# A decoder step with 32 experts: rows of the expert matrices dealt to the partitions in blocks of eight

## The chip, the cores and the metric

The kernel runs on one core of one Trainium2 chip. The metric is the device time of one execution in microseconds (us), taken as the median of several runs. TensorE is written PE, its weight load PEld, VectorE DVE, ScalarE ACT, GpSimd POOL and the engine that issues most DMAs SP.

## The reference, cut to what matters

One step of a decoder trunk: 256 prompt tokens and 8 sample tokens, 264 in all, of width 1024. Attention and a gated linear attention come first, then a mixture of experts with 32 experts, of which each token uses 4. All numbers are float32. What bears on the change is the expert part:

```python
def expert_ffn(xb, w_gu, b_gu, w_d, b_d):
    gu = xb @ w_gu + b_gu                 # xb (rows, 1024), w_gu (1024, 2048)
    gate, up = jnp.split(gu, 2, axis=-1)
    gate = jnp.minimum(gate, SWIGLU_LIMIT)
    up = jnp.clip(up, -SWIGLU_LIMIT, SWIGLU_LIMIT)
    glu = gate * jax.nn.sigmoid(SWIGLU_ALPHA * gate)
    return ((up + 1) * glu) @ w_d + b_d   # w_d (1024, 1024)
```

Both products sum over 1024 rows of a weight matrix. The order in which these rows are taken does not matter, as long as the other operand is taken in the same order.

## The kernel before, in words

The program is written engine by engine, with semaphores. A first phase (to about 424 us of the trace) computes attention and the projections, with the layer's other weights. The second phase is the expert part, and all of its weights, 32 x 12 MB, pass once through `ring`, six slots of 2 MB in SBUF.

**Loads.** SP issues them (`load_expert`, L1719 to L1732): for each expert four loads of `w_gu` and two of `w_d`, 2 MB each, in the order in which PE uses them. Each waits at `slots_used` until PE has finished with the slot. The 1024 rows of a matrix are cut as "(k p)": block k holds 128 consecutive rows, one to a partition. A `w_gu` load takes two blocks, so a partition gets two separate rows of 8 KB; a `w_d` load takes four blocks, so a partition gets four separate rows of 4 KB.

**Routing.** After the second norm (`normed`, L1192 to L1206) the activations stand in `hT` with the 1024 features on the partitions. PE turns them into token rows (L737 to L742, the helper `transpose` at L337), in six banks of PSUM, two of which are in use in turn, and ACT copies each bank to `tok` (`copy_out`, L1061 to L1063 and L953). In PE's order behind these turns come the small matmuls that count the tokens of each expert (L744 to L755), which DVE waits for to make `pick` (`set_pick`, L1535 to L1543), the 0/1 matrix that says which token stands in which of an expert's 64 places.

**Experts, in pairs.** `gather` (L771 to L779) multiplies `tok`, 128 features at a time, with `pick` and so gives `xg`, the tokens of two experts with the features on the partitions. `gate_up` (L786 to L813) multiplies `xg` with the `w_gu` slots: two column halves of the array work at once, one for gate and one for up. DVE and ACT make the SwiGLU (`swiglu`, L1554 to L1566) and leave it in `hid`, 64 rows of 1024 features. `turn_hidden` (L815 to L823) turns it: eight matmuls, each with 128 columns of `hid` as weights and the 64 x 64 identity as moving operand. ACT copies the result to `hidT` (L1080). `down` (L833 to L847) multiplies `hidT` with the `w_d` slots; `combine` (L849 to L857) puts the rows back to their tokens and DVE adds them to `acc` (L1572). PE's order is written out by hand in `pair` (L859 to L888), so that the steps of one expert stand between the matmuls of another.

**The end.** A last norm (L1638 to L1646), turns, and the stores of y.

A float32 matmul shows in the trace as two instructions of weight load and two of matmul; a `transpose` shows as one of each.

Of the kernel before, what the change touches and what calls it, by code (L numbers as in the profile page):

```python
# [29 lines left out]
ACT = mybir.ActivationFunctionType  # L30
AX_X = mybir.AxisListType.X

P = 128
D = 1024
KT = D // P
# [9 lines left out]
NE, TOPK, FF = 32, 4, 1024  # L45
CAP = 64
# [34 lines left out]
def decoder_step(nc, x_prompt, x_sample, c_prompt, c_sample, cache_k, cache_v, cache_logf, state_gla,  # L81
# [4 lines left out]
    with ExitStack() as ctx:  # L86
# [7 lines left out]
        ps = ctx.enter_context(nc.psum_tensor("ps", [P, 8, 512], F32))  # L94
# [19 lines left out]
        tok = sb("tok", [P, 3, D])  # L114
# [67 lines left out]
        hid = part(zone, slice(0, CAP), 4160, FF)  # L182
# [60 lines left out]
        scalar_full, scalar_free = sem("scalar_full"), sem("scalar_free")  # L243
# [9 lines left out]
        v_index, a_index, q_index = {}, {}, {}  # L253
# [47 lines left out]
        def _(pe):  # L301
# [41 lines left out]
            bank = vector_bank()  # L343
# [3 lines left out]
            bank = vector_bank()  # L347
            for k in range(KT):
                ins = transpose(bank[:, 9 * k:9 * k + 9], c_rows[:, k * P:(k + 1) * P])
# [3 lines left out]
            for k in range(KT):  # L353
                bank = vector_bank()
                for t, (t0, tn) in enumerate(TOK_TILES):
                    ins = transpose(bank[:, t0:t0 + tn], tok[0:tn, t, k * P:(k + 1) * P])
# [36 lines left out]
            bank = vector_bank()  # L393
            for t, (t0, tn) in enumerate(TOK_TILES):
                ins = pe.matmul(bank[:, t0:t0 + tn], ones[0:tn, :], rstd_diag[0:tn, t, 0:tn],
                                start=True, stop=True)
# [35 lines left out]
            bank = vector_bank()  # L432
            from_scalar("q3")
            for i in range(4):
                ins = transpose(bank[0:NS, i * P:(i + 1) * P], qT[:, i, TP:T])
# [12 lines left out]
            for name, src in (("k", kT), ("v", vT)):  # L448
                from_scalar(f"{name}3")
                for t, (t0, tn) in enumerate(TOK_TILES):  # L450
                    bank = vector_bank()
                    for i in range(4):
                        ins = transpose(bank[0:tn, i * P:(i + 1) * P], src[:, i, t0:t0 + tn])
# [4 lines left out]
            bank = vector_bank()  # L458
            for t, (t0, tn) in enumerate(TOK_TILES):
                transpose(bank[0:tn, t * HA:(t + 1) * HA], fT[:, t0:t0 + tn])  # L460
            for t in range(2):
                ins = transpose(bank[:, (3 + t) * HA:(4 + t) * HA], neg_cum[0:HA, t * P:(t + 1) * P])
# [3 lines left out]
            bank = vector_bank()  # L466
            pe.matmul(bank[:, 0:HA * NS], ones[:, :], qk_new.rearrange("p a b -> p (a b)"), start=True, stop=True)
            ins = pe.matmul(bank[:, HA * NS:2 * HA * NS], ones[0:NS, :], f_diag.rearrange("p a b -> p (a b)"),
                            start=True, stop=True)
# [62 lines left out]
            for i in range(2):  # L532
                bank = vector_bank()
                vector_filled(pe.matmul(bank[:, 0:T], w_alpha_sb[:, i * P:(i + 1) * P], alrT[:, :],
                                        start=True, stop=True), f"alpha{i}")
            for c in range(NCH):
                bank = scalar_bank()
                for h in range(HB):
                    ins = transpose(bank[0:CH, h * DV:(h + 1) * DV], vbT[:, h, c * CH:(c + 1) * CH])
                scalar_filled(ins, f"vb_tok{c}")  # L540
            bank = vector_bank()
            for h in range(HB):
                ins = transpose(bank[0:NS, h * DV:(h + 1) * DV], vbT[:, h, TP:T])
# [6 lines left out]
            for i in range(2):  # L550
                for f in range(2):
                    half = slice(64 * f, 64 * f + 64)
                    bank = vector_bank()
                    for c in range(NCH):
                        ins = pe.matmul(bank[0:CH, c * CH:(c + 1) * CH], e_k[half, i * NCH + c, :],
                                        e_q[half, i * NCH + c, :], start=True, stop=True)
# [3 lines left out]
            bank = vector_bank()  # L560
            for h in range(HA):
                ins = transpose(bank[:, h * 64:(h + 1) * 64], lf_rows[:, h:h + HA * (PAGE - 1) + 1:HA])
# [4 lines left out]
            for i in range(2):  # L567
                bank = scalar_bank()
                for c in range(NCH):
                    ins = transpose(bank[0:CH, c * P:(c + 1) * P], al_d[:, i * NCH + c, :])  # L570
                scalar_filled(ins, f"kd_tok{i}")
            from_scalar("kd_tok1")
            for i in range(2):
                for c2 in range(2):
                    bank = vector_bank()
                    for c in (2 * c2, 2 * c2 + 1):
                        ins = pe.matmul(bank[:, (c % 2) * 256:(c % 2) * 256 + 256], kd_tok[:, i, c, :],
                                        vb_tok[:, c, i * 256:(i + 1) * 256], start=True, stop=True)
# [5 lines left out]
            for h in range(HB):  # L584
                i, f = h // 2, h % 2
                bank = vector_bank()
                for c in range(NCH):
                    ins = pe.matmul(bank[:, c * CH:(c + 1) * CH], vb_tok[:, c, h * DV:(h + 1) * DV],
                                    A_T[:, i, f, c * CH:(c + 1) * CH], start=True, stop=(c == 0))
                    if c:  # L590
                        ins = pe.matmul(bank[:, c * CH:(c + 1) * CH], gla_S[:, c - 1, i, :],
                                        qe[:, f, i * NCH + c, :], start=False, stop=True)
# [4 lines left out]
            bank = vector_bank()  # L597
            vector_filled(pe.matmul(bank[:, :], ones[:, :], past_lf.rearrange("p a b -> p (a b)"),
                                    start=True, stop=True), "page_sums")
            bank = vector_bank()  # L600
# [16 lines left out]
            for b in range(NS):  # L617
                if b in (3, 6):
                    gate_tile()
                bank = vector_bank()  # L620
# [5 lines left out]
            bank = vector_bank()  # L626
            out = bank[:, 0:64].rearrange("p (i f b) -> p i f b", i=2, f=2, b=16)[:, :, :, 0:NS]
            for b in range(NS):
                for i in range(2):
                    ins = pe.matmul(out[:, i, :, b], state[:, b, i, :], qb_new[:, i, b, :],  # L630
                                    start=True, stop=True)
# [5 lines left out]
            for h in range(HB):  # L637
                bank = vector_bank()
# [5 lines left out]
            bank = vector_bank()  # L644
# [3 lines left out]
            bank = vector_bank()  # L648
# [3 lines left out]
            bank = vector_bank()  # L652
# [33 lines left out]
            bank = vector_bank()  # L686
            for i in range(4):
                ins = transpose(bank[:, i * NS:(i + 1) * NS], o_rows[:, i * P:(i + 1) * P])
# [6 lines left out]
            for m in range(KT):  # L695
                for n, src in enumerate((oT[:, :, :], obT)):
                    bank = vector_bank()
                    for k in range(4):
                        ins = pe.matmul(bank[:, 0:T], wb[n][:, k, m * P:(m + 1) * P], src[:, k, :],  # L699
                                        start=(k == 0), stop=(k == 3))  # L700
# [8 lines left out]
            for m in range(KT):  # L709
                bank = vector_bank()  # L710
                for k in range(KT):
                    ins = pe.matmul(bank[:, 0:T], wo[k // 4][:, k % 4, m * P:(m + 1) * P], hT[:, k, :],  # L712
                                    start=(k == 0), stop=(k == KT - 1))
# [12 lines left out]
            bank = vector_bank()  # L726
            for k in range(KT):
                pe.wait_ge(sig("h2T"), k + 1)
                ins = pe.matmul(bank[0:NE, 0:T], w_r[:, k, :], hT[:, k, :], start=(k == 0), stop=(k == KT - 1))
            vector_filled(ins, "logitsT")  # L730
            from_vector("logitsT")
            bank = vector_bank()
            for t, (t0, tn) in enumerate(TOK_TILES):
                ins = transpose(bank[0:tn, t * NE:(t + 1) * NE], logitsT[:, t0:t0 + tn])
            vector_filled(ins, "logits")

            for t, (t0, tn) in enumerate(TOK_TILES):  # L737
                for g in range(2):
                    bank = scalar_bank()
                    for k in range(4):  # L740
                        ins = transpose(bank[0:tn, k * P:(k + 1) * P], hT[:, 4 * g + k, t0:t0 + tn])
# [3 lines left out]
            bank = vector_bank()  # L745
# [69 lines left out]
            def turn_hidden(n, j, first):  # L815

                pe.wait_ge(sig("hid_ready"), 2 * n + j + 1)
                if not first:
                    pe.wait_ge(sig("turn_read"), 3 * n + j)
                for k in range(KT):  # L820
                    ins = pe.matmul(ps[:, 4, k * CAP:(k + 1) * CAP], hid[:, k * P:(k + 1) * P],  # L821
                                    ident[0:CAP, 0:CAP], start=True, stop=True)
                ins.then_inc(sig("turned"), 1)  # L823

# [101 lines left out]
        def _(act):  # L926
# [21 lines left out]
            def copy_out(dst, name, rows=P, cols=T, func=ACT.Copy, scale=1.0):  # L948
                bank = take(name)
                src = bank[0:rows, 0:cols]  # L950
                if len(dst.shape) == 3:
                    src = src.rearrange("p (a b) -> p a b", b=dst.shape[2])
                nc.scalar.activation(dst, src, func, scale=scale).then_inc(scalar_free, 1)  # L953
# [106 lines left out]
            squares_and_root("x1", "x1_sq", "x1_ss", "x1_rms")  # L1060
            for t, (t0, tn) in enumerate(TOK_TILES):  # L1061
                for g in range(2):
                    copy_out(tok[0:tn, t, g * 512:(g + 1) * 512], f"h2_tok{t}{g}", rows=tn, cols=512)  # L1063
            act.wait_ge(sig("top_shift"), 1)
            nc.scalar.activation(logits, logits, ACT.Exp).then_inc(sig("top_exp"), 1)

# [583 lines left out]
        def _(sp):  # L1650
# [62 lines left out]
                    store(logf_prompt[0, 0].rearrange("(t p) h -> p t h", p=P), f_tok[:, 0:2, :])  # L1713
                    store(logf_sample[0].rearrange("b s h -> (b s) h"), f_tok[0:NS, 2, :])

            gu = w_gu[0].rearrange("e (k p) c -> e p k c", p=P)
            dn = w_d[0].rearrange("e (k p) c -> e p k c", p=P)

            def load_expert(kind, e, number, edge, phase_one=False):  # L1719

# [119 lines left out]
```

## Time and profile before

| what | value |
|---|---|
| median of 3 runs | 1529.31 us (1526.75 to 1529.6) |
| span of the profiled execution | 1524.6 us |
| own time of the profiled execution | not given apart from its span |
| PE busy | 1426.3 us, 94% |
| PE weight load busy | 714.7 us, 47% |
| DVE, ACT, POOL busy | 472.4, 197.6 and 25.3 us |
| mean granted clock of PE | 0.961 of 2.4 GHz |
| DMA | 497.75 MB, mean 326 GB/s |

The span runs from the first to the last instruction of the profiled execution; the runs' times also hold what lies around it, 4.7 us if the profiled execution is like the median run. "Busy" for PE counts pipelined matmuls, which overlap, so 94% says that PE hardly stands still, and not that it works at its peak. The time lies in two phases: about 424 us of the first, and from there to 1524.6 us the routing, the experts and the end.

### The profile page before, as it was taken

The page shows a single profiled execution, that of the slowest core. Times are in us where ns is not written, and L with a number is a line of the kernel's source. Part 1 is how long each engine was busy: PE and PEld are TensorE (multiplying, and loading weights), DVE is VectorE, ACT ScalarE, POOL GpSimd, SP SyncE. Part 2 cuts the span into 40 slices and gives each one's busy share as a digit, 9 for nine tenths or more (in the row PEclk, how much of TensorE's full clock was granted, in tenths as well). Part 3 has the DMA queues.
Part 4 walks back from the last instruction along what each step waited for, and adds up shares of the span by engine and source line. Part 5 has one row for each costly group of instructions (what it writes and reads, how often), then busy time and mean ns, then how long its engine had stood idle before and what let it go on. Part 6 is the DMA issues. An engine that isn't in the chain of part 4 may idle for free.

```text
span 1524.6 us, 17634 instructions
## 1 busy us (share of the span) xinstructions
PE 1426.3 (94%) x6765; PEld 714.7 (47%) x6765; DVE 472.4 (31%) x919; ACT 197.6 (13%) x334; POOL 25.3 (2%) x53
## 2 busy tenths in 40 slices
PE   5999789997979999999999999999999999999996
PEld 2876457645853443434344343443434344343433
DVE  3278764412232141221223122141221322222133
ACT  1022400200120111011011111111101011111112
POOL 0000010210000000000000000000000000000000
PEclk9999967998978999999999999999999999999998
DMA  9935754788426898999999999899998989989980
GB/s 355 332 119 197 284 177 155 275 326 336 133 103 268 366 418 366 364 416 364 420 365 397 382 365 418 365 419 364 364 417 363 418 366 380 400 363 418 367 324 30
DMA packets 103927, 497.75 MB, mean 326 GB/s; under 512 B 6257, under 2 KB 6367, under 8 KB 68016
## 3 DMA queue, kind: packets, MB, share of 16 engines
q1 hardware_dynamic: 100464, 486.77, 80.0%
q0 software_dynamic: 3152, 10.37, 1.9%
q8 instruction: 24, 0.39, 0.1%
q10 hardware_dynamic: 272, 0.09, 0.0%
q14 instruction: 15, 0.12, 0.0%
HBM read 493.86 MB, written 3.35 MB: 326 GB/s over the span
## 4 chain that ended last, share of the span: by engine, by line
PE 85%; DVE 7%; DMA 4%; issue 2%; ACT 2%; DVEq 0%; ACTq 0%; SPq 0%
PE ps L805 29%; PE ps L844 15%; PE ps L776 9%; PE ps L410 9%; PE ps L856 5%; PE ps L821 4%; PE ps L794 4%; PE ps L699 2%; PE ps L712 2%; DMA ring<-in_w_in 2%; DMA ring<-in_w_branch 2%; PE ps L337 1%; PE ps L667 1%; DVE ring L1221 1%; DVE zone L1549 1%
## 5 line engine op out<-in xcount | busy, mean ns | idle before, releaser
L805 PE MATMUL ps<-ring,zone 128*64 128x512 f32 x2048 | 471.0, 603 | 0.0
L805 PEld LDWEIGHTS ps<-ring,zone 128*64 128x64 f32 x2048 | 136.8, 137 | 270.3 <-issue 267.9
L844 PE MATMUL ps<-ring,oT 128*64 128x512 f32 x1024 | 226.0, 594 | 0.0
L1557 DVE TENSOR_SCALAR zone<-ps 64x1024 f32<-64x1024 f32 x32 | 38.9, 1217 | 499.7 <-PE ps L805 499.7
L410 PE MATMUL ps<-hT,ring 128*128 128x264 f32 (+2 forms) x672 | 166.6, 407 | 2.8 <-DMA ring<-in_w_in 2.8
L410 PEld LDWEIGHTS ps<-hT,ring 128*128 128x128 f32 (+2 forms) x672 | 129.7, 196 | 41.8 <-issue 9.7
L776 PE MATMUL ps<-zone,tok 128*128 128x128 f32 (+1 forms) x768 | 142.7, 318 | 2.5 <-DVE zone L1541 2.5
L844 PEld LDWEIGHTS ps<-ring,oT 128*64 128x64 f32 x1024 | 72.1, 137 | 138.9 <-issue 137.0
L776 PEld LDWEIGHTS ps<-zone,tok 128*128 128x128 f32 (+1 forms) x768 | 109.0, 195 | 45.3 <-issue 18.2
L1572 DVE TENSOR_TENSOR zone<-zone,ps 128x264 f32<-128x264 f32 x128 | 53.6, 428 | 174.6 <-PE ps L856 173.3
L856 PE MATMUL ps<-zone,v_tok 128*128 128x264 f32 x256 | 74.1, 412 | 24.1 <-DVE zone L1572 22.6
L856 PEld LDWEIGHTS ps<-zone,v_tok 128*128 128x128 f32 x256 | 43.0, 188 | 80.4 <-issue 37.3
L1080 ACT ACTIVATE oT<-ps 128x512 f32<-128x512 f32 x32 | 19.1, 597 | 385.9 <-PE ps L821 385.9
L821 PEld LDWEIGHTS ps<-ident,zone 64*128 64x128 f32 x512 | 59.4, 188 | 19.0 <-issue 19.0
L821 PE MATMUL ps<-ident,zone 64*128 64x64 f32 x512 | 63.9, 275 | 0.0
L794 PE MATMUL ps<-zone 32*64 32x512 f32 x256 | 63.6, 614 | 0.0
L1090 ACT ACTIVATE v_tok<-ps 64x512 f32<-64x512 f32 x64 | 37.8, 591 | 176.5 <-PE ps L844 176.1
L1076 ACT ACTIVATE k_tok<-zone 64x1024 f32<-64x1024 f32 x32 | 33.8, 1057 | 174.1 <-DVE zone L1557 174.1
L1538 DVE COPY zone<-ident 32x64 f32 (+1 forms) x32 | 5.7, 179 | 125.1 <-PE ps L805 125.1
L953 ACT ACTIVATE zone<-ps 128x264 f32<-128x264 f32 (+1 forms) x41 | 15.9, 387 | 186.5 <-PE ps L410 186.5
L1559 DVE TENSOR_SCALAR zone<-ps 64x1024 f32<-64x1024 f32 x32 | 39.2, 1226 | 1.0
L1562 DVE SCALAR_TENSOR_TENSOR zone<-zone 64x1024 f32<-64x1024 f32 x32 | 38.9, 1217 | 1.1
(281 smaller groups left out, 864.4 us busy)
## 6 DMA issues: line engine op xcount, KB each, us to landing
ring<-in_w_gu SPq DMA_DIRECT2D x128, 2048.0 KB, 10.4
ring<-in_w_d SPq DMA_DIRECT2D x64, 2048.0 KB, 12.4
ring<-in_w_ada SPq DMA_DIRECT2D x12, 2048.0 KB, 13.2
ring<-in_w_in SPq DMA_DIRECT2D x8, 2048.0 KB, 16.1
ring<-in_cache_k SPq DMA_DIRECT2D x64, 256.0 KB, 3.6
ring<-in_cache_v POOLq DMA_DIRECT2D x32, 256.0 KB, 6.1
ring<-in_cache_v SPq DMA_DIRECT2D x32, 256.0 KB, 6.2
ring<-in_w_branch SPq DMA_DIRECT2D x2, 2048.0 KB, 22.2
```

Source lines behind the costliest of these rows:

```text
L410: ins = pe.matmul(bank[0:width, 0:T], w[:, k, c0:c0 + width], hT[:, k, :], start=(k == 0), stop=(k == KT - 1))
L776: ins = pe.matmul(out, tok[0:tn, t, k * P:(k + 1) * P], pick[0:tn, t, :], start=(t == 0), stop=(t == 2))
L794: pe.matmul(banks[64 * half:64 * half + CAP, c, :], expert_row[:, j, :], b_gu_rows[:, half * FF + c * 512:half * FF + (c + 1) * 512], star ...
L805: ins = pe.matmul(banks[64 * half:64 * half + CAP, c, :], xg[:, k, j * CAP:(j + 1) * CAP], w[:, kk, half * FF + c * 512:half * FF + (c + 1 ...
L821: ins = pe.matmul(ps[:, 4, k * CAP:(k + 1) * CAP], hid[:, k * P:(k + 1) * P], ident[0:CAP, 0:CAP], start=True, stop=True)
L844: ins = pe.matmul(ps[64 * half:64 * half + CAP, 5, :], hidT[:, k, :], w[:, kk, half * 512:(half + 1) * 512], start=(k == 0), stop=(k == KT ...
L856: pe.matmul(ps[:, 6 + m % 2, 0:T], ye_tok[:, m * P:(m + 1) * P], putT, start=True, stop=True).then_inc(sig("combined"), 1)
L1090: ins = nc.scalar.activation(ye_tok[64 * j:64 * j + CAP, half * 512:(half + 1) * 512], ps[64 * half:64 * half + CAP, 5, :], ACT.Copy)
L1557: V.tensor_scalar(gate_v, ps[0:CAP, 2 * j:2 * j + 2, :].rearrange("p a b -> p (a b)"), LIMIT, None, ALU.min).then_inc(sig("gate_ready"), 1)
L1559: V.tensor_scalar(hid, ps[64:64 + CAP, 2 * j:2 * j + 2, :].rearrange("p a b -> p (a b)"), LIMIT, -LIMIT, ALU.min, ALU.max).then_inc(sig("u ...
L1562: V.scalar_tensor_tensor(out=hid, in0=hid, scalar=1.0, in1=gate_v, op0=ALU.add, op1=ALU.mult)\
L1572: V.tensor_tensor(acc[:, m, :], acc[:, m, :], ps[:, 6 + m % 2, 0:T], ALU.add)\
```

## The change

It has three parts that belong together.

1. **The loads.** The rows of an expert's matrices are cut as "(p k)" in place of "(k p)": partition p holds the eight consecutive rows 8p to 8p + 7. A `w_gu` load of two k then takes two consecutive rows of 8 KB for a partition, 16 KB in a row, and a `w_d` load of four k takes four consecutive rows of 4 KB, also 16 KB in a row. In the compiled program the load of either kind becomes 128 partitions x 4096 elements, in place of 128 x 2 x 2048 and 128 x 4 x 1024. From one partition to the next the address steps by 64 KB in `w_gu` and 32 KB in `w_d`. The number, size and order of the loads and their waits stay.
2. **`tok`.** Block k of `xg` must now hold the features 8p + k. ACT's copies of the turned activations write the features in that order: `by_row` sends feature 128k + 8b + r to place 128r + 16k + b. An instruction reads its 512 numbers from PSUM in a row and writes them to SBUF in steps of 512 B, eight at a time. The slices of `tok` that `gather` reads stay contiguous.
3. **`hid`.** `turn_hidden` takes for block k every eighth column, from k on, as weights: 128 numbers of a partition with a step of 32 B, in place of 128 in a row.

The output of the experts keeps its order, since only rows that are summed over move. PE's, DVE's and POOL's instructions keep their order and shapes.

```diff
@@ turn_hidden
                 for k in range(KT):
-                    ins = pe.matmul(ps[:, 4, k * CAP:(k + 1) * CAP], hid[:, k * P:(k + 1) * P],
+                    ins = pe.matmul(ps[:, 4, k * CAP:(k + 1) * CAP], hid[:, k:FF - KT + k + 1:KT],
                                     ident[0:CAP, 0:CAP], start=True, stop=True)
@@ ACT, after squares_and_root("x1", ...)
                 for g in range(2):
-                    copy_out(tok[0:tn, t, g * 512:(g + 1) * 512], f"h2_tok{t}{g}", rows=tn, cols=512)
+                    by_row = tok[0:tn, t, :].rearrange("p (r k b) -> p k b r", r=KT, k=KT)
+                    act.wait_ge(scalar_full, a_index[f"h2_tok{t}{g}"])
+                    bank = ps[0:tn, (a_index[f"h2_tok{t}{g}"] - 1) % 2, :]
+                    nc.scalar.activation(by_row[:, 4 * g:4 * g + 4, :, :],
+                                         bank.rearrange("p (k b r) -> p k b r", k=4, r=KT), ACT.Copy)\
+                        .then_inc(scalar_free, 1)
@@ SP
-            gu = w_gu[0].rearrange("e (k p) c -> e p k c", p=P)
-            dn = w_d[0].rearrange("e (k p) c -> e p k c", p=P)
+            gu = w_gu[0].rearrange("e (p k) c -> e p k c", p=P)
+            dn = w_d[0].rearrange("e (p k) c -> e p k c", p=P)
```

## Rows read from the trace of the kernel before

**Rows 1.** The page, part 1: busy time, share and instructions of each engine.

```profile
span 1524.6 us, 17634 instructions
PE 1426.3 (94%) x6765; PEld 714.7 (47%) x6765; DVE 472.4 (31%) x919; ACT 197.6 (13%) x334; POOL 25.3 (2%) x53
```

**Rows 2.** Waits in 475:1480, PE alone: engine line <- releaser: us, times, longest.

```profile
PE ps L856 <- DVE zone L1572: 22.6, 14, 1.6
PE ps L767 <- DVE zone L1624: 1.5, 1, 1.5
```

**Rows 3.** Waits of SP's own queue in 500:1480, same columns.

```profile
SPq L1731 <- PE ps L805: 555.1, 119, 6.0
SPq L1731 <- PE ps L844: 298.4, 60, 11.4
```

**Rows 4.** Windows: stretch, us, busy PE PEld DVE ACT POOL, PEclk, DMA share, GB/s.

```profile
500.00:1480.00 980.00, 957.40 (x4631) 409.40 (x4629) 237.57 (x445) 109.88 (x166) 0.00 (x0) 1.00 0.95 386
920.00:950.00 30.00, 28.39 (x130) 10.13 (x126) 10.00 (x24) 2.63 (x4) 0.00 (x0) 1.00 1.02 417
20.00:25.00 5.00, 3.93 (x18) 2.02 (x22) 1.36 (x6) 0.00 (x0) 0.00 (x0) 1.00 1.01 419
```

**Rows 5.** The page, parts 3 and 6: two DMA queues, and the expert loads' issues.

```profile
q1 hardware_dynamic: 100464, 486.77, 80.0%
q8 instruction: 24, 0.39, 0.1%
...
ring<-in_w_gu SPq DMA_DIRECT2D x128, 2048.0 KB, 10.4
ring<-in_w_d SPq DMA_DIRECT2D x64, 2048.0 KB, 12.4
```

**Rows 6.** Line L821, the turn of `hid`: count, ns min/median/max, first and last start.

```profile
L821 PEld LDWEIGHTS ps<-ident,zone x512: 182/188/188, 494.6 to 1485.6; 64*128 64x128 f32 x171
L821 PE MATMUL ps<-ident,zone x512: 272/272/320, 494.6 to 1485.6; 64*128 64x64 f32 x171
```

**Rows 7.** Timeline, 32 gate/up matmuls and one turn of `hid`: start, us, what.

```profile
917.12 7.09 PE L805 MATMUL ps<-ring,zone 128*64 128x512 f32 x32
...
949.24 1.86 PEld L821 LDWEIGHTS ps<-ident,zone 64*128 64x128 f32 x16 [0.34 <-issue]
```

**Rows 8.** Tile gla_S at L337, weights with a step of 8 floats; its timeline; its window.

```profile
L337 PEld LDWEIGHTS ps<-ident,gla_S x8: 182/203/204, 195.0 to 195.8; 64*128 64x128 f32 x8
...
195.05 0.96 PEld L337 LDWEIGHTS ps<-ident,gla_S 64*128 64x128 f32 x8
...
195.00:196.00 1.00, 1.00 (x10) 0.95 (x8) 0.84 (x2) 0.00 (x0) 0.00 (x0) 0.50 0.00 0
```

**Rows 9.** Lines L667 (weights with a step) and L674 (in a row), and their timeline.

```profile
L667 PEld LDWEIGHTS ps<-ring,dec_scores x128: 91/99/138, 282.8 to 331.3; 128*8 128x8 f32 x128
L674 PEld LDWEIGHTS ps<-tok,small x16: 86/90/90, 290.7 to 333.1; 128*8 128x8 f32 x16
...
325.28 0.14 PEld L667 LDWEIGHTS ps<-ring,dec_scores 128*8 128x8 f32 x7 [0.34 <-issue]
...
326.13 0.09 PEld L667 LDWEIGHTS ps<-ring,dec_scores 128*8 128x8 f32 x1 [0.34 <-issue]
```

**Rows 10.** The chain of waits from 431.98 to 439.46: start, us, what.

```profile
431.98 0.61 ACT tok L953
...
433.32 0.61 ACT tok L953
...
433.97 1.09 PE ps L337 x8
435.06 0.14 PE ps L750 x2
...
439.46 15.03 PE ps L776 x48
```

**Rows 11.** Timeline of ACT, the third pair of copies; a later gather on PE.

```profile
434.61 1.08 ACT L953 ACTIVATE tok<-ps 8x512 f32<-8x512 f32 x2 [0.20 <-PE ps L337]
...
957.71 8.51 PE L776 MATMUL ps<-zone,tok 128*128 128x128 f32 x48
```

**Rows 12.** Windows, columns as in rows 4: the first gather and what follows it.

```profile
440.00:450.00 10.00, 10.00 (x35) 7.53 (x33) 0.78 (x4) 0.60 (x1) 0.00 (x0) 0.50 0.00 0
450.00:460.00 10.00, 10.00 (x29) 4.79 (x30) 0.00 (x0) 1.88 (x2) 0.00 (x0) 0.50 0.01 2
```

## The prediction

> **What bounds the kernel now.** I read the engine shares first, then the waits of the expert phase, then its windows. PE is busy for 94% of the span and no other engine for more than 31% [rows 1]. That alone would allow for a phase in which the DMAs are the bound, so the waits of the experts' stretch come next. From 475 to 1480 us PE's matmuls wait for another unit 15 times, 24.1 us in all, each time for DVE; no DMA stands in that list [rows 2]. The opposite holds: SP, which issues the loads, waits 555.1 + 298.4 = 853.5 of 980 us for PE to give slots back [rows 3]. The loads follow PE, not PE the loads.
>
> How near the loads are to being the bound is in the windows [rows 4]. Over 980 us the experts take 386 GB/s with the DMA engines busy at a share of 0.95; where the engines are full (share 1.02) they move 417 GB/s, and 419 GB/s near the start, with rows of 8 KB that lie 24 KB apart. So PE asks for 386 / 417 = 93% of what the DMAs give. The stretch is PE's, with some 7% in hand for the DMAs: a faster load buys nothing, a load slower by more than 7% costs.
>
> **The change part by part.** The sum is made against the profiled execution, whose span is 1524.6 us; the median of the runs is 1529.31 us. I put the difference of 4.7 us down to what lies around the span and add every term to the median. About 3 us, 0.2%, is what a measurement of this kernel can tell from no change; the three runs lie 2.85 us apart.
>
> *Loads: 192 instructions, neither more nor fewer, same order, same waits.* There are 128 + 64 of 2 MB each [rows 5], 402.7 MB. Their pieces grow from 8 KB and 4 KB to 16 KB. If the longer pieces are moved faster, the gain lies beside PE's work: each load lands earlier in a slot that PE comes to later, and SP's 853.5 us of waiting grow. Worth 0 us, and the cover is PE itself; nothing in this change shortens PE's work, so the cover stays. If they are moved slower, up to 7% is hidden too. The trace holds 24 packets of 16 KB, code loads on queue 8: 0.39 MB in 0.1% of 16 engines' span, which by the rounding is anything between 0.5 and 1.5 us for one [rows 5]. At 417 GB/s over 16 engines, 16 KB take 0.63 us. That row is too coarse and lies on another queue, so the near rows are the two at 417 and 419 GB/s, which agree although in one the rows stand 24 KB apart and in the other they follow each other. I take 0, with +28 us as the far end (a rate 10% lower, worked out under the rivals). Below nothing the reason above excludes a gain.
>
> *The turn of `hid`: 512 weight loads and 512 matmuls [rows 6], all on PE, all on the path.* This is the term to look at hardest, because PE has no slack. One turn is 16 weight loads in 1.86 us [rows 7]: less the last one's own 0.188 us, (1.86 - 0.188) / 15 = 0.111 us from one to the next, or 0.87 ns for each of 128 columns. The weight load sets this pace and not the matmul: 32 matmuls of 512 columns, two at a time, take 7.09 us [rows 7], which is 0.44 us for 512 columns and 0.055 us for the 64 of the identity. So each ns that a stepped read adds to a weight load counts 512 times.
>
> The trace has the same read already. Line L562 turns `lf_rows` with every eighth column as weights, 64 x 128 floats with a step of 32 B, just what the change reads. These are the eight loads on gla_S [rows 8]: (0.96 - 0.203) / 7 = 0.108 us from one to the next, 0.85 ns a column, at a granted clock of 0.50, that is 1.2 GHz. A cycle of 1.2 GHz is 0.83 ns, so this is about a column a cycle. The stepped read thus kept up with a column every 0.85 ns, and the turn of `hid` asks for one every 0.87 ns. I take 0 us. What remains open is that those eight are single-pass turns at the lower clock level, and these are float32 matmuls at the higher one. The row with a step at the higher clock is L667, eight columns 256 B apart: median 99 ns against 90 ns for eight columns in a row at L674 [rows 9]. Taken at face value that is 1.1 ns a column, 144 ns a load, 512 x 0.144 = +74 us. I don't take it: L667's loads come in bursts of seven and eight, where one stands behind another, and one that comes alone takes 0.09 us like L674's [rows 9]. Both ends stay for the range: 0 and +74 us.
>
> The rows above show no penalty at one column every 0.85 ns. The Trainium skill (SBUF — State Buffer, section "Door 1: The DMA port swizzle") says otherwise: memory lines are 16 B, a reader needs at least two hits on a line to run at full rate, and float32 can be stepped for free by four numbers at most. By that rule the turn would slow down with its step of eight, and the sum would go up by the first rival's price; by the row it stays at 0.
>
> *ACT's six copies to `tok`.* Each takes 0.6 us now, and writes 512 numbers in a row. The trace has no ACT copy that writes in steps of 512 B, so I bound it: nothing below, since the count and the PSUM side are unchanged, and a doubling above (+0.6 us each). Their place on the path is in the chain of waits [rows 10]: with two banks in turn, the last turns of PE need the fourth copy, and the small matmuls of the counts (from 435.06) stand behind them in PE's queue; DVE waits for those. A doubling thus costs 4 x 0.6 = +2.4 us. The last two copies [rows 11] end at 435.7, while the gather that needs them starts at 439.46 [rows 10], so they are covered even then. I take 0, the value of the same copy in a row, since in PSUM, where the copy begins, nothing changes; +2.4 stays in the range.
>
> *The gather and the gate/up and down matmuls* read `tok`, `xg`, `hidT` and the slots in rows as before: 0.
>
> Sum: 0 + 0 + 0 + 0 us. Predicted 1529.3 us, no change.
>
> **The rivals.**
>
> *1. The stepped weight read takes double (slower).* For it: the step leaves each 16 B line after one number, and L667's median. Against it: the eight loads on gla_S. Price: a column at 1.74 in place of 0.87 ns, 512 x 0.111 = +57 us, 1586 us. It decides as soon as a stepped column needs more than 0.87 ns; each 0.1 ns over that costs 512 x 128 x 0.1 ns = 6.6 us. Chance 0.08.
>
> *2. The loads become the bound (slower).* 16 KB from each of 128 places 64 KB or 32 KB apart could be served more slowly than pieces that follow each other. It decides below 386 GB/s, 7% under today's full rate. At 375 GB/s, 10% under, the stretch of 980 us becomes 980 x 386 / 375, +28 us, 1557 us, and waits of PE for `ring` appear. Against it: 419 GB/s with rows 24 KB apart [rows 4]. Chance 0.04. The Trainium skill (DMA: Bandwidth & Descriptors, section "Latency and other measured facts") has such a rule: rows of 16 KiB at a pitch that is a large power of two are copied at 207 GB/s with 512 KiB and 164 with 2 MiB, against 214 with a padded pitch. It gives nothing for 64 KB; by its 512 KiB value, an estimate, 3% would be lost and the 7% would cover it. No row here shows a pitch of a power of two with separate places.
>
> *3. ACT's copies slow down by more than double (slower).* Three times over is +4.8 us, 1534 us. Chance 0.03.
>
> *4. The clock (faster).* From 440 to 460 us PE is granted 0.50 [rows 12], after a stretch in which it waited much for DVE and ACT; the first gather takes 15.03 us [rows 10] where a later one takes 8.51 [rows 11]. If the clock stayed up there, the gather alone would give back 6.5 us: 1523 us. Nothing in the change shortens the waits ahead of it. Chance 0.04.
>
> *5. The change doesn't do what it says.* The loads could be cut into the old pieces on the way. The time is that of the forecast. Chance 0.02.
>
> **How the numbers follow.** The forecast has 0.79; of that I give 0.03 to a measurement that falls below by over 0.2% and 0.02 to one above. Faster: 0.04 + 0.03 = 0.07. Slower: 0.08 + 0.04 + 0.03 + 0.02 = 0.17. Same: 0.76. The range reaches from 1525 (1.75 under the lowest run, 1526.75) to 1537 (2.4 us of copies, rival 3, and a first part of rival 1 up to 0.1 ns a column). Rivals 1, 2 and 4 at their prices stay out, 0.16 together.
>
> **What would show it.** Right: the weight loads of the turn at 188 ns and 1.86 us for 16; SP still waiting for PE over 850 us; no wait of PE for `ring`; packets under 8 KB in queue 1 fewer by about 32768; the six copies near 0.6 us. Wrong: a turn of `hid` longer than 2 us, a DMA among PE's releasers after 475 us, or a PE stretch at another clock level than before.

## The result and the profile after

The changed kernel takes 1651.0 us (median of 4, 1649.82 to 1652.1), the kernel before 1528.99 us. The ratio is 1.0809 with a 95% interval of 1.0793 to 1.0825: 122 us slower, where no change was forecast and the range ended at 1537 us.

The page of the changed kernel, parts 1 and 3, against [rows 1] and [rows 5]:

```profile
span 1648.8 us, 17634 instructions
PE 1549.9 (94%) x6765; PEld 793.2 (48%) x6765; DVE 472.6 (29%) x919; ACT 200.4 (12%) x334; POOL 25.4 (2%) x53
...
q1 hardware_dynamic: 59504, 486.77, 73.4%
```

The counts are the old ones; PE's busy time grew by 123.6 us and that of its weight loads by 78.5 us, DVE's by nothing. Queue 1 moved the same 486.77 MB in 40960 packets fewer, so the loads do what the change says. Its share of the engines' span fell from 80.0% to 73.4%, but mostly because the span grew: 80.0% of 1524.6 us is 1220 us, 73.4% of 1648.8 us is 1210 us. The groups of section 5 that moved:

```profile
L805 PE MATMUL ps<-ring,zone 128*64 128x512 f32 x2048 | 524.8, 660 | 0.0
...
L844 PE MATMUL ps<-ring,oT 128*64 128x512 f32 x1024 | 228.0, 598 | 0.0
...
L821 PEld LDWEIGHTS ps<-ident,zone 64*128 64x128 f32 x512 | 124.3, 331 | 19.0 <-issue 19.0
...
L821 PE MATMUL ps<-ident,zone 64*128 64x64 f32 x512 | 129.5, 406 | 0.0
```

Two things stand in them. The turn of `hid` (L821) has weight loads of 331 ns where [rows 6] have a median of 188, and 129.5 us of matmul busy time, where the kernel before had 63.9. And the gate/up matmuls (L805), which the change doesn't touch, have a mean of 660 ns where it was 603, 53.8 us more of busy time. The down matmuls (L844), equally untouched, are up by 2 us only. What sets L805 apart is seen in time order. This is the timeline of PE in the changed kernel (start, us, what) around one turn, to be held against [rows 7]:

```profile
967.73 1.40 PE L821 MATMUL ps<-ident,zone 64*128 64x64 f32 x5
969.06 8.48 PE L805 MATMUL ps<-ring,zone 128*64 128x512 f32 x32
977.47 0.59 PE L337 MATMUL ps<-ident,zone 128*128 128x128 f32 x3
```

and these its windows, columns as in [rows 4]:

```profile
960.00:965.00 5.00, 5.00 (x24) 1.44 (x20) 0.00 (x0) 0.00 (x0) 0.00 (x0) 1.00 1.01 433
965.00:969.00 4.00, 4.00 (x18) 3.88 (x16) 0.00 (x0) 0.00 (x0) 0.00 (x0) 0.94 1.02 430
969.00:972.00 3.00, 3.00 (x9) 1.00 (x10) 0.00 (x0) 0.60 (x1) 0.00 (x0) 0.52 0.65 279
972.00:976.00 4.00, 4.00 (x20) 1.26 (x18) 0.00 (x0) 0.00 (x0) 0.00 (x0) 1.00 0.62 201
...
500.00:1600.00 1100.00, 1077.53 (x4646) 484.23 (x4647) 237.54 (x445) 110.69 (x167) 0.00 (x0) 0.94 0.84 344
```

The same 32 matmul instructions take 8.48 us instead of 7.09, because at the end of the turn (965.06 to 969.06) PE falls to its lower level, 0.50 or 1.2 GHz, for some 3 us. The experts' stretch has a mean clock of 0.94 where [rows 4] have 1.00. Added up over the clock's record in the trace, PE had no stretch at 0.50 between 490 us and the end of the experts before, and now has 31, 130 us in all. (One stretch from 483 to 490 us stands in both kernels.) The waits are what they were: PE's matmuls for DVE only, SP for PE.

```profile
PE ps L856 <- DVE zone L1577: 22.5, 14, 1.6
PE ps L767 <- DVE zone L1629: 1.5, 1, 1.5
```

```profile
SPq L1736 <- PE ps L805: 678.6, 120, 9.7
SPq L1736 <- PE ps L844: 300.8, 60, 11.5
```

A sum of where the 124.2 us of span lie, by the first and last start of the turn in line L821's row:

```profile
L821 PEld LDWEIGHTS ps<-ident,zone x512: 308/332/334, 496.1 to 1607.5; 64*128 64x128 f32 x171
```

The first turn begins at 496.1 instead of 494.6 [rows 6], 1.5 us later; from the first turn to the last it is 1111.4 instead of 991.0 us, 120.4 us more; behind the last, 41.3 instead of 39.0 us. Of the 120.4, a turn that takes 4.05 instead of 2.00 us (means of all 32) gives 32 x 2.05 = 66 us, and 54 us are left for the clock. All 32 turns count, since the last start in the row is that of the last turn's last load. The 54 us fit the clock's record: 111 of the 130 us at 0.50 fall on L805's matmuls, which run at half their pace there and so lose 56 us, and 14 us fall on the turns themselves, whose loads turn out below to take the same time at both levels.

The three theories at this point. **A**: all of it comes from the stepped read of `hid`, about half directly and half because the slower turn brings the clock down. **B**: the 16 KB pieces or the reordered copies to `tok` carry a part. **C**: the clock falls after any turn that takes so long. Later runs add rivals to parts of A.

### The profile page after: what moved, and what is told of

It reads as the page before. It is cut to its first block, busy times and chain, and to the rows that moved or that the text cites. A ratio compares the mean times of both kernels' runs of the same rounds, so it can differ in the third digit from the quotient of the medians.

```text
span 1648.8 us, 17634 instructions
## 1 busy us (share of the span) xinstructions
PE 1549.9 (94%) x6765; PEld 793.2 (48%) x6765; DVE 472.6 (29%) x919; ACT 200.4 (12%) x334; POOL 25.4 (2%) x53
## 3 DMA queue, kind: packets, MB, share of 16 engines
q1 hardware_dynamic: 59504, 486.77, 73.4%
## 4 chain that ended last, share of the span: by engine, by line
PE 86%; DVE 6%; DMA 3%; issue 2%; ACT 2%; DVEq 0%; ACTq 0%; SPq 0%
PE ps L805 30%; PE ps L844 14%; PE ps L776 9%; PE ps L410 8%; PE ps L821 8%; PE ps L856 4%; PE ps L794 4%; PE ps L699 2%; PE ps L712 2%; DMA ring<-in_w_in 1%; DMA ring<-in_w_branch 1%; PE ps L337 1%; PE ps L667 1%; DVE ring L1226 1%; DVE zone L1554 1%
## 5 line engine op out<-in xcount | busy, mean ns | idle before, releaser
L805 PE MATMUL ps<-ring,zone 128*64 128x512 f32 x2048 | 524.8, 660 | 0.0
L805 PEld LDWEIGHTS ps<-ring,zone 128*64 128x64 f32 x2048 | 149.4, 150 | 312.1 <-issue 308.9
L844 PE MATMUL ps<-ring,oT 128*64 128x512 f32 x1024 | 228.0, 598 | 0.0
L844 PEld LDWEIGHTS ps<-ring,oT 128*64 128x64 f32 x1024 | 72.6, 138 | 140.4 <-issue 138.6
L821 PEld LDWEIGHTS ps<-ident,zone 64*128 64x128 f32 x512 | 124.3, 331 | 19.0 <-issue 19.0
L821 PE MATMUL ps<-ident,zone 64*128 64x64 f32 x512 | 129.5, 406 | 0.0
L1571 DVE TENSOR_TENSOR zone<-zone,k_tok 64x1024 f32<-64x1024 f32 x32 | 38.9, 1217 | 1.1
```

The lines of the kernel that those rows point to most:

```text
L805: ins = pe.matmul(banks[64 * half:64 * half + CAP, c, :], xg[:, k, j * CAP:(j + 1) * CAP], w[:, kk, half * FF + c * 512:half * FF + (c + 1 ...
L821: ins = pe.matmul(ps[:, 4, k * CAP:(k + 1) * CAP], hid[:, k:FF - KT + k + 1:KT], ident[0:CAP, 0:CAP], start=True, stop=True)
L844: ins = pe.matmul(ps[64 * half:64 * half + CAP, 5, :], hidT[:, k, :], w[:, kk, half * 512:(half + 1) * 512], start=(k == 0), stop=(k == KT ...
L1571: V.tensor_tensor(hid, hid, sig_v, ALU.mult).then_inc(sig("hid_ready"), 1)
```

## The experiments

### Only w_gu, and only w_d

`a_gu_only` is the change less these two lines, `b_dn_only` the kernel before with them:

```diff
-ins = pe.matmul(ps[:, 4, k * CAP:(k + 1) * CAP], hid[:, k * P:(k + 1) * P], ...
+ins = pe.matmul(ps[:, 4, k * CAP:(k + 1) * CAP], hid[:, k:FF - KT + k + 1:KT], ...
-dn = w_d[0].rearrange("e (k p) c -> e p k c", p=P)
+dn = w_d[0].rearrange("e (p k) c -> e p k c", p=P)
```

> Only w_gu is dealt in blocks of eight rows, with the reordered copies to tok; w_d and the turn of hid are as before. Theory A (all of the loss hangs on the stepped weight read of hid): 1529 us plus the 1.3 us by which the slower copies delay the first gather, 1530 us; no granted clock of 0.50 between 490 and 1485 us; the gate/up loads still move in packets of 16 KB. Rival B (the 16 KB pieces or the copies carry part of the 122 us): two thirds of the pieces are there, so up to 1610 us.

> Only w_d is dealt in blocks of eight rows, with the stepped read of hid; w_gu and the copies to tok are as before. Theory A: 1650 us less 1.3 us, 1649 us, weight loads of the turn at 332 ns and some 120 us of granted clock 0.50 after 490 us. Rival B: a third of the 16 KB pieces, so clearly under 1649 us.

Measured: `a_gu_only` 1527.6 us against 1527.79, ratio 1.0003 (0.9993 to 1.0012). `b_dn_only` 1647.02 us, ratio 1.0785 (1.0762 to 1.0809), with weight loads of the turn at 308/332/334 ns. Its clock record has 130 us at 0.50 in the experts; that of `a_gu_only` has none but the stretch before 492 us that the kernel before has too. B falls as a source of any large part: two thirds of the 16 KB pieces and the six slower copies cost nothing that can be measured, and without them nearly the whole loss is there. What is left between 1647 and 1651 us is of the size of the copies' term and a measurement's noise.

### Which step costs

`c_steps` is the kernel before with the eight matmuls of each turn on eight lines, with steps 1 to 8:

```diff
-for k in range(KT):
-    ins = pe.matmul(ps[:, 4, k * CAP:(k + 1) * CAP], hid[:, k * P:(k + 1) * P], ...
+ins = pe.matmul(ps[:, 4, 0:64], hid[:, 0:0+1*127+1:1], ...
+ins = pe.matmul(ps[:, 4, 64:128], hid[:, 0:0+2*127+1:2], ...
...
+ins = pe.matmul(ps[:, 4, 448:512], hid[:, 0:0+8*127+1:8], ...
```

> The kernel before, but the eight matmuls of each turn read hid with steps of 1, 2, 3, 4, 5, 6, 7 and 8 numbers, each on a line of its own; the experts' output is not the reference's, the amount of work is. Theory A1 (the cost is per number that opens another 16 B line, as the Trainium skill, SBUF - State Buffer, has it: four numbers of step are free): 188 ns at steps 1 to 4, 332 ns at 5 to 8. Theory A2 (two hits on a line are needed): 188 ns at 1 and 2, 332 ns from 4 on, 3 between them. Theory A3 (any step other than 1 costs the same): 332 ns from 2 on.

The weight loads of its lines, step 1 at L820 to step 8 at L834, ns min/median/max:

```profile
L820 PEld LDWEIGHTS ps<-ident,zone x64: 182/184/186, 495.2 to 1567.3; 64*128 64x128 f32 x64
...
L822 PEld LDWEIGHTS ps<-ident,zone x64: 192/193/195, 495.4 to 1567.5; 64*128 64x128 f32 x64
...
L824 PEld LDWEIGHTS ps<-ident,zone x64: 248/254/260, 495.7 to 1567.8; 64*128 64x128 f32 x64
...
L826 PEld LDWEIGHTS ps<-ident,zone x64: 314/320/327, 496.0 to 1568.2; 64*128 64x128 f32 x64
...
L828 PEld LDWEIGHTS ps<-ident,zone x64: 312/314/316, 496.5 to 1568.6; 64*128 64x128 f32 x64
...
L834 PEld LDWEIGHTS ps<-ident,zone x64: 330/331/332, 497.8 to 1570.0; 64*128 64x128 f32 x64
```

Step 2 costs 9 ns a load, step 3 costs 70, step 4 costs 136, and from there it hardly grows (steps 6 and 7: 316 and 322). The cost is there nearly in full from a step of four on, as it would be if memory gave out lines of four numbers, 16 B: a step of two then finds two numbers in each line, one of three finds one or two, one of four finds one. A2 fits all eight steps, with 314 to 331 ns in place of 332 from four on; A1 and A3 do not: two numbers have to come from a line. The Trainium skill (SBUF — State Buffer, section "Door 1: The DMA port swizzle") says both things in one paragraph, that two hits on a line are needed and that float32 may be stepped by four for free. The runs bear out the first and contradict the second: four costs nearly what eight does (320 ns against 331). The kernel took 1612.05 us in its one run.

### The same length of turn without a step

`d_double` makes each turn twice, with `hid` read in a row:

```diff
-for k in range(KT):
+for k in [*range(KT), *range(KT)]:
```

> The kernel before, but each turn of hid is made twice, in a row, so that it takes as long as the stepped turn (about 3.8 us against 4.07) with weight loads that run at their usual pace; the result is the same. Theory A with a cost of time alone: 32 x 1.79 = 57 us, 1586 us, and the granted clock stays at 1.00 between 490 and 1485 us. Rival C (the clock falls after any turn of that length, however the weights are read): 57 us and some 61 us for stretches at 0.50, 1647 us.

Measured 1635.46 us, ratio 1.071 (1.0686 to 1.0733). Its windows around one double turn (958.1 to 961.8):

```profile
958.00:962.00 4.00, 4.00 (x36) 3.84 (x36) 0.00 (x0) 0.10 (x1) 0.00 (x0) 1.00 1.03 423
962.00:966.00 4.00, 4.00 (x12) 1.12 (x10) 0.00 (x0) 0.50 (x1) 0.00 (x0) 0.57 0.68 285
966.00:970.00 4.00, 4.00 (x22) 1.29 (x18) 0.00 (x0) 0.00 (x0) 0.00 (x0) 1.00 0.92 297
```

C is right on the clock: it falls after a double turn of 3.78 us though no weight read is stepped. The record has 26 stretches at 0.50, 109 us. The two terms, 32 x 1.78 = 57 us and 109 / 2 = 55 us, make 112; measured are 108. (Half of the 109 us is a little too much, since not all of them fall on matmuls that lose half their pace.) So the stepped read costs through its time, and the clock is a second cost of that time. The run also shows the turn's loads in a row at both levels: 188 ns at 1.00, and up to 335 ns where the clock was at 0.50:

```profile
L821 PEld LDWEIGHTS ps<-ident,zone x1024: 182/188/335, 495.9 to 1594.3; 64*128 64x128 f32 x171
```

The stepped loads of the changed kernel have the same 332 ns at both levels. The step costs a time in ns, which at 1.2 GHz nearly disappears behind the clock: there a load in a row starts 0.213 us after the last (`d_double`), a stepped one 0.238 us.

### Single-pass turns, with and without the step

`e_step8_transpose` (on the changed kernel) and `f_transpose` (on the kernel before) put single-pass turns in the place of seven of the eight matmuls:

```diff
-    ins = pe.matmul(ps[:, 4, k * CAP:(k + 1) * CAP], hid[...], ident[0:CAP, 0:CAP], ...)
+    if k:
+        ins = transpose(ps[:, 4, k * CAP:(k + 1) * CAP], hid[...])
+    else:
+        ins = pe.matmul(ps[:, 4, k * CAP:(k + 1) * CAP], hid[...], ident[0:CAP, 0:CAP], ...)
```

> The change, but seven of the eight float32 matmuls of each turn of hid are single-pass turns (transpose), still with the step of eight; the first stays. Theory A4 (memory gives a reader that leaves its line one number every 0.9 ns at either clock level, and a float32 weight load reads each column twice): the stepped single-pass loads start 0.11 us apart at 2.4 GHz as they did at 1.2 GHz, a turn takes 0.5 + 7 x 0.11 = 1.3 us, the clock stays up, and the kernel takes 1528 - 32 x 0.7 + 1.3 = 1507 us. Rival D (a step costs 144 ns a load whatever the pass): 0.2 us apart, a turn of 1.9 us, 1528 us.

> The kernel before with the same edit, hid read in a row: loads 0.06 us apart, a turn of 0.22 + 7 x 0.06 = 0.6 us in place of 2.0, 1528 - 32 x 1.4 = 1483 us if PE's time is all that counts; more if PE then waits for DMAs, since the loads have only 7% in hand and this takes 3% of it.

Measured: `e_step8_transpose` 1509.9 us, ratio 0.988 (0.9864 to 0.9897); `f_transpose` 1495.07 us, ratio 0.9785 (0.9769 to 0.9802). The timeline of one turn's weight loads, first in `e_step8_transpose`:

```profile
944.92 0.55 PEld L824 LDWEIGHTS ps<-ident,zone 64*128 64x128 f32 x2 [0.34 <-issue]
...
945.21 1.02 PEld L337 LDWEIGHTS ps<-ident,zone 64*128 64x128 f32 x7
```

and in `f_transpose`:

```profile
964.82 0.29 PEld L824 LDWEIGHTS ps<-ident,zone 64*128 64x128 f32 x2 [0.81 <-issue]
...
964.98 0.57 PEld L337 LDWEIGHTS ps<-ident,zone 64*128 64x128 f32 x7
```

The single records inside the first of these groups read 203 ns each and start 0.110 to 0.113 us apart, as seven of the eight stepped loads on gla_S do at 1.2 GHz (0.110 to 0.111 us in their single records behind [rows 8]), and now at 2.4 GHz. The stepped float32 loads of the changed kernel start 0.238 us apart, a little over twice that. Rival D (0.2 us apart whatever the pass) falls, A4 holds in its numbers: a stepped number takes about 0.87 ns at either clock level, and a float32 weight load of 128 columns behaves as if it read 256 numbers. That it reads each column twice is inferred from the two paces and not seen.

`e_step8_transpose` is 3 us above its 1507. `f_transpose` missed its 1483 by 12 us. A turn there takes 0.87 us in place of 2.00, and not the 0.6 that I had reckoned with: 32 x 1.13 = 36 us, which is 1492. Some 3 us more are lost behind the experts, in all four kernels with the single-pass turn: PE waits 6.8 to 7.3 us ahead of the last norm's sums (L720), and 3.6 to 4.2 us in the other nine. No run shows why. The clock stayed up through the experts, until 3.4 us at 0.50 behind the last turn. PE's share of DMA waits stayed at nil, although the engines were at 0.98 (windows, 500 to 1440 us):

```profile
500.00:1440.00 940.00, 917.40 (x4391) 373.42 (x4389) 233.97 (x440) 108.83 (x165) 0.00 (x0) 1.00 0.98 400
```

### The layout kept, the stepped read moved or made smaller

`g_dve_writes` lets DVE write the last product of SwiGLU in the order of the blocks, so that PE reads in a row; `gate_v` is free by then:

```diff
-V.tensor_tensor(hid, hid, sig_v, ALU.mult).then_inc(sig("hid_ready"), 1)
+V.tensor_tensor(gate_v.rearrange("p (k q) -> p q k", k=KT),
+                hid.rearrange("p (q k) -> p q k", k=KT),
+                sig_v.rearrange("p (q k) -> p q k", k=KT), ALU.mult).then_inc(...)
-... hid[:, k:FF - KT + k + 1:KT] ...
+... gate_v[:, k * P:(k + 1) * P] ...
```

`h_step2` deals `w_d` in pairs of rows, on the kernel before:

```diff
-... hid[:, k * P:(k + 1) * P] ...
+... hid[:, 2 * P * (k // 2) + k % 2:2 * P * (k // 2) + 2 * P - 1 + k % 2:2] ...
-dn = w_d[0].rearrange("e (k p) c -> e p k c", p=P)
+dn = w_d[0].rearrange("e (b p k) c -> e p b (k c)", p=P, k=2)
-src, k = dn[bass.ds(e, 1), :, 4 * s:4 * s + 4, :], 4
+src, k = dn[bass.ds(e, 1), :, 2 * s:2 * s + 2, :], 2
```

> The change, but DVE's last product of SwiGLU writes its 1024 numbers in the order of the blocks (to gate_v, with a step of 128 numbers), and the turn reads them in a row. Theory A (the whole loss is the stepped weight read): weight loads at 188 ns, no stretch at 0.50 between 490 and 1485 us, 1529 us. DVE's product may take up to 2.4 us in place of 1.22, which its idle time covers. Rival B (16 KB pieces of w_d cost): over 1532 us.

> The kernel before with w_d alone dealt in pairs of rows (partition p of a block of 256 has rows 2p and 2p + 1), so its loads have pieces of 8 KB and the turn reads hid with a step of two. By c_steps a step of two costs 5 to 9 ns a load: 512 x 7 ns = 3.6 us at most, 1528 to 1532 us, no stretch at 0.50. Rival: a turn longer by 0.1 us is enough to bring the clock down, 1580 us or more.

Measured: `g_dve_writes` 1531.91 us, ratio 1.0024 (1.0014 to 1.0034); `h_step2` 1531.89 us, ratio 1.0027 (1.0016 to 1.0037). With all the 16 KB pieces and all the copies in place, and only PE's read mended, 118 of the 122 us are gone. That settles A against B. Of the 4 us that `g_dve_writes` still loses, the trace places none in the loop: from the first turn to the last it is 991.0 us, as before.

```profile
L821 PEld LDWEIGHTS ps<-ident,zone x512: 182/188/188, 497.6 to 1488.6; 64*128 64x128 f32 x171
```

They lie before the first turn (497.6 instead of 494.6 us) and behind the last. Before the first: the copies to `tok` hold up the first gather by 1.3 us; DVE's product, which now takes 1.95 instead of 1.22 us, is waited for once, ahead of L767 (2.1 us of wait instead of 1.5); and a stretch at 0.50 lasts 10.2 instead of 6.8 us. Behind the last: a stretch at 0.50 from 1490.2 us, in which 32 down matmuls take 8.77 instead of 7.09 us. Two single traces are compared here, and runs of one kernel lie up to 4.5 us apart, so this split is no more than what the traces show. In `h_step2` the loads take 193 instead of 188 ns and a turn 2.09 instead of 2.00 us, 32 x 0.1 = 3 us of its 4.0; its clock record has 3.4 us at 0.50 more than the kernel before, behind the last turn.

### The turn in two halves

`k_split` is the changed kernel, every stepped read in place, but four matmuls of the turn stand at one place in PE's order and four at the next, with 16 gate/up instructions between:

```diff
-if k == 4:
-    turn_hidden(n, 0, cold)
+if k >= 4:
+    turn_hidden(n, 0, cold, range(2 * k - 8, 2 * k - 4))
...
-if k == 2:
-    turn_hidden(n, 1, False)
+if k in (2, 4):
+    turn_hidden(n, 1, False, range(2 * k - 4, 2 * k))
```

> The change, with each turn of hid in two halves of four matmuls, 16 gate/up matmul instructions apart (the last pair's second turn stays whole); every stepped weight read is still there, so the direct cost of 66 us stays. Theory A (the other half of the loss is the clock, which falls after PE has spent 4 us in one go on the turn): the stretches at 0.50 between 485 us and the end of the experts go, and the kernel takes 1528 + 66 + 2 = 1596 us. Rival E (the clock's fall comes with the stepped reads however they are spread): 1645 to 1655 us, some 125 us at 0.50.

Measured 1602.79 us, ratio 1.0503 (1.0486 to 1.0521). The clock's record has two stretches at 0.50 in the experts, 10 us, where the changed kernel has 130 us, and the longer one (6.8 us from 1558.0) begins in the one turn that stays whole, the last. One half and what follows it on PE:

```profile
950.57 2.12 PE L822 MATMUL ps<-ident,zone 64*128 64x64 f32 x8
952.62 3.65 PE L805 MATMUL ps<-ring,zone 128*64 128x512 f32 x16
```

16 gate/up instructions take 3.65 us, their time at the upper level. The direct term is 32 x (2 x 2.12 - 2.00) = 72 us, and with 5 us for the clock that makes 77; 76 are measured. Rival E falls: it is the 4 us in one go that bring the clock down, not the stepped reads as such. Of the changed kernel's 122 us of loss, 46 go away by the order alone.

### The layout with a faster turn

`i_dve_writes_transpose` is `g_dve_writes`, and `j_gu_transpose` is `a_gu_only`, each with the single-pass turn of `f_transpose`.

> g_dve_writes (16 KB pieces everywhere, DVE writes hid in the order of the blocks) with f_transpose's single-pass turn. If PE's time is all that counts: 1532 - 33 = 1499 us. If the 16 KB pieces are worth something now that the DMA engines are at a share of 0.98 in f_transpose: down to 1493 us, and a share clearly under 0.98.

> a_gu_only (16 KB pieces for w_gu alone, hid in a row) with f_transpose's single-pass turn: 1495 us, f_transpose's time, if the DMAs stay hidden, since a_gu_only was at the kernel before within 0.1%; under 1494 us if the DMAs had begun to hold PE in f_transpose.

Measured 1497.05 us (ratio 0.9811, 0.9794 to 0.9827) and 1497.04 us (0.9805, 0.9788 to 0.9821), some 2 us from the 1499 and 1495 us expected for loads that stay hidden. The windows of `i_dve_writes_transpose`, against the row of `f_transpose` above:

```profile
500.00:1440.00 940.00, 917.41 (x4391) 373.50 (x4389) 255.86 (x440) 108.60 (x165) 0.00 (x0) 1.00 0.95 400
```

At the same 400 GB/s the engines are busy at 0.95 instead of 0.98. So the longer pieces are moved in about 3% less time, and even here, where PE asks for 4% more than before, it buys nothing, since PE waits for no load in either. The lowest median of all is that of `f_transpose`, which has none of the change: 1495.07 us, 32.9 under its own runs of the kernel before. Its ratio's interval overlaps those of the two above.

## Why the prediction was wrong

Point by point, by its own steps.

- **What bounds the kernel**: right. PE is the bound before and after, and SP's loads follow it.
- **Loads, 0 us**: right, shown by `a_gu_only` and `g_dve_writes`. The queue got 2 to 4% cheaper (median 611 ns for a 16 KB piece in the trace's packet records; before, 312 for one of 8 KB and 159 for one of 4 KB), and it stayed hidden.
- **The turn of `hid`, 0 us**: wrong, and this is the step that failed. The prediction said "The stepped read thus kept up with a column every 0.85 ns, and the turn of `hid` asks for one every 0.87 ns." It set a single-pass load beside a float32 one and counted both in columns. The paces in `e_step8_transpose` and in the changed kernel, 0.111 and 0.238 us for the same 128 columns, show that a float32 load asks for twice as much. Against the limit of the row on gla_S it asked for a number every 0.43 ns, twice what that row had delivered. The rows held a warning: 0.87 ns a column are two cycles of 2.4 GHz, while the single-pass loads on gla_S took one cycle of 1.2 GHz a column, so the two forms did not work alike. (`f_transpose` shows a single-pass load in a row at 2.4 GHz: 0.06 us from one to the next, where a float32 one takes 0.111.)
- **L667, set aside**: the 74 us that this row gave came near the direct cost: the starts of the loads moved from 0.111 to 0.238 us apart, 512 x 0.127 = 65 us. The prediction said "Both ends stay for the range: 0 and +74 us" and then gave a range that ends at +8, which was a mistake of its own. That the row's 144 ns a load are also the measured 332 - 188 ns is luck. In the trace of the kernel before, at the upper level, 12 loads of L667 stand alone and take 91 to 94 ns, against 90 for L674's, while the 100 in bursts have a median of 99. So most of the 9 ns belongs to the bursts, as the prediction held, and the row was weak evidence for a price.
- **The rule on memory lines**: what the Trainium skill (SBUF — State Buffer, section "Door 1: The DMA port swizzle") says of two hits on a line spoke against the change and was right in direction. The prediction put an observation at another level of the clock and in another pass above it, and gave its first rival 0.08.
- **Rival 1's price**: the mechanism, with its place and its point of decision, was right; +57 us was too small twice over. The direct term is 66 us. And the clock was missing: the prediction treated it only as a rival on the faster side. Its signs of being wrong named a PE stretch at another clock level, but no term of the sum and no rival priced one. Its fall costs some 54 us more.
- **ACT's copies**: inside their bounds. The chain in the changed kernel has the four copies in one piece,

```profile
432.92 3.72 ACT tok L1066 x4
...
436.69 0.60 PE ps L337 x4
...
441.68 3.58 PE ps L776 x11
```

  with 1.05 us for a copy that took 0.6, and the first gather 8.76 us after the first copy instead of 7.48 [rows 10], 1.3 us later.
- **Rivals 2 to 5**: none came about.
- **The 4.7 us put down to what lies around the span**: in the changed kernel's profiled execution these are 1.4 us (1650.17 us against a span of 1648.8). The profiled execution of the kernel before was thus some 3 us quicker than the median run; the forecast did not hang on it.

What stays open: why PE's clock falls after such a turn and not after the first version of it. The runs show that 3.8 to 4.1 us of turn in one go were followed by the fall in most cases (31 of 32 turns in the changed kernel, 26 of 32 in `d_double`), that a turn of 3.3 us in `c_steps` was too (26 stretches), and that turns or halves of turns of 2.0 to 2.1 us were not, stepped or in a row, but for one stretch among the 62 halves of `k_split`. Open as well: why the last norm starts 3 us later behind a single-pass turn.

## What to carry to other kernels

When rows of a matrix are dealt to the partitions in blocks, the other operand must be read or written with a step somewhere; before anything else, ask which engine pays for it, and put it on one with idle time (DVE here) and not in the weight reads of a PE that never waits. Longer DMA pieces are worth nothing while the queue waits for slots that PE gives back, as the 7% in hand said here. And a read seen at a lower clock level, or in another pass of the same instruction, is no bound for the read at the upper one: compare numbers per ns that each form really takes, and price what a longer light stretch does to PE's clock.

## What the runs showed of the hardware that was not expected

- A weight load of 128 float32 columns at 2.4 GHz takes 184 ns in a row, 193 with a step of 2, 254 with 3, 320 with 4 and 331 with 8 (`c_steps`).
- The stepped read, with a step of 8, has a pace in ns and not in cycles: 332 ns and 0.238 us apart for the float32 loads at 2.4 and at 1.2 GHz (the changed kernel), 203 ns and 0.111 us apart for single-pass ones at both (`e_step8_transpose`, and gla_S in the kernel before).
- PE's granted clock fell at 31 of 32 turns of 4.05 us among matmuls that kept PE without a gap, and stayed up in all but one case when the same turns were cut in two (`k_split`). PE was busy in 4.00 of 4.00 us where it fell (965 to 969 us of the changed kernel), so a PE without gaps can still lose the upper level.
- An ACT copy of 512 numbers that writes in steps of 512 B takes 1.05 us where one in a row takes 0.6 (the changed kernel), and DVE's product of 1024 that writes with a step of 128 numbers takes 1.95 where it took 1.22 (`g_dve_writes`).
